# Another fixed order for the 524 interleaved steps of the hybrid mixer

## What is computed

```python
def hybrid_mixer(h, ...):
    proj = h @ w_in
    gq, gk, gv, gate, ga, gb, sq, sk, sv = _split(proj, HYB_SPLITS)
    qkv = causal_short_conv(concat(gq, gk, gv), conv_w)      # 4 heads of 128
    o_a = gated_delta_rule(l2_norm(q), l2_norm(k), v, g, beta)
    o_a = rms_norm(o_a, gdn_norm) * silu(gate)
    o_b = stick_breaking_attention(rms_norm(sq), rms_norm(sk), sv)   # 8 heads of 64
    return concat(o_a, o_b) @ w_out
```

## Time and profile before

| | us |
|---|---|
| runs of the kernel: lowest, median, highest (3 runs) | 2892.62, 2895.24, 2897.87 |
| profiled execution, its span (first to last instruction) | 2890.9 |
| of it the mixer on PE, from its first slab to the output projection | 41.4 to 445.0 |
| the four mixer parts used below | 40 to 155, 155 to 265, 265 to 360, 360 to 445 |

### The profile page before, as it was taken

How to read it: one execution, slowest core, us unless ns; L and a number is a source line. 1 busy time by engine, 2 the same in 40 slices (tenths; PEclk the granted TensorE clock), 3 DMA queues, 4 the chain that set the end, 5 groups by cost and what they waited for, 6 DMA issues and landing times.

```text
span 2890.9 us, 31908 instructions
## 1 busy us (share of the span) xinstructions
PE 2779.2 (96%) x13258; PEld 2203.1 (76%) x13258; DVE 1412.4 (49%) x2062; ACT 961.1 (33%) x1264; POOL 547.4 (19%) x422
## 2 busy tenths in 40 slices
PE   7998989999999999999999999899999998999998
PEld 4776657888887787788888876688888875788886
DVE  6645546666545333373222455555345465454453
ACT  3435444322233322243222333433223344322222
POOL 2563301100112201221001200022012100121121
PEclk9999979999999999999999999899999999999999
DMA  6322103446322222223632322122322321222321
GB/s 242 124 92 93 50 8 146 175 174 226 142 99 99 91 79 86 77 88 102 173 116 70 121 93 71 38 106 84 108 102 71 120 62 62 73 98 79 108 84 69
DMA packets 51089, 296.28 MB, mean 102 GB/s; under 512 B 6618, under 2 KB 6746, under 8 KB 25089
## 3 DMA queue, kind: packets, MB, share of 16 engines
q1 hardware_dynamic: 44912, 276.58, 27.1%
q0 software_dynamic: 4736, 15.34, 2.0%
q10 hardware_dynamic: 1296, 2.32, 0.2%
HBM read 283.46 MB, written 8.65 MB: 101 GB/s over the span
## 4 chain that ended last, share of the span: by engine, by line
PE 88%; DVE 5%; ACT 4%; issue 1%; POOL 1%; DMA 0%; SPq 0%; DVEq 0%
PE ps L218 87%; DVE wlo L211 1%; PE ps L1327 1%; ACT whi L200 1%; DMA F<-in_ada 0%; ACT F L1344 0%; DVE F L418 0%; DVE hl L422 0%; DVE ada L466 0%; DVE F L2270 0%; ACT L253 0%; ACT E L2843 0%; DVE F L833 0%; ACT E L2841 0%; ACT hh L436 0%
## 5 line engine op out<-in xcount | busy, mean ns | idle before, releaser
L218 PE MATMUL ps<-hh,whi 128*128 128x512 f32 x2088 | 829.1, 397 | 12.6 <-ACT F L2821 5.8
L218 PE MATMUL ps<-hl,whi 128*128 128x512 f32 x2088 | 814.9, 390 | 0.0
L218 PE MATMUL ps<-hh,wlo 128*128 128x512 f32 x2088 | 813.9, 390 | 0.0
L211 DVE TENSOR_TENSOR wlo<-raw,whi 128x2048 fp32r<-128x2048 f32 (+2 forms) x235 | 496.2, 2111 | 503.5 <-ACT whi L200 501.3
L218 PE MATMUL ps<-R,whi 128*128 128x512 f32 x2080 | 651.3, 392 | 8.0 <-DVE wlo L211 3.1
L200 ACT ACTIVATE whi<-raw 128x2048 fp32r<-128x2048 f32 (+2 forms) x235 | 409.7, 1744 | 746.8 <-PE ps L218 746.7
L218 PEld LDWEIGHTS ps<-hh,whi 128*128 128x128 f32 x2088 | 392.8, 188 | 103.6 <-issue 12.2
L218 PEld LDWEIGHTS ps<-R,whi 128*128 128x128 f32 x2080 | 391.1, 188 | 95.7 <-issue 6.9
L218 PEld LDWEIGHTS ps<-hl,whi 128*128 128x128 f32 x2088 | 392.6, 188 | 83.4
L218 PEld LDWEIGHTS ps<-hh,wlo 128*128 128x128 f32 x2088 | 393.1, 188 | 82.1 <-issue 3.3
L218 PE MATMUL ps<-R,wlo 128*128 128x512 f32 x1040 | 405.2, 390 | 0.0
(11 more groups left out here) (341 smaller groups left out, 2434.7 us busy)
## 6 DMA issues: line engine op xcount, KB each, us to landing
F<-in_ada SPq DMA_DIRECT2D x32, 1024.0 KB, 4.8
raw<-in_fs0in SPq DMA_DIRECT2D x22, 1024.0 KB, 5.5
raw<-in_fs1in SPq DMA_DIRECT2D x22, 1024.0 KB, 4.8
raw<-in_fc0in SPq DMA_DIRECT2D x22, 1024.0 KB, 4.8
raw<-in_fc1in SPq DMA_DIRECT2D x22, 1024.0 KB, 4.8
Rf<-in_ada0h SPq DMA_DIRECT2D x24, 512.0 KB, 3.5
raw<-in_fs0out SPq DMA_DIRECT2D x16, 704.0 KB, 4.3
raw<-in_fs1out SPq DMA_DIRECT2D x16, 704.0 KB, 4.3
```

Of the source, the lines that this page charges most:

```text
L211: e.tensor_tensor(m.wlo[n % 2][:, 0:size], m.raw[m.slot[n]][:, 0:size], m.whi[n % 2][:, 0:size].bitcast(F32), SUB).then_inc(*s.up("wlo", n))
L218: return e.matmul(out, l, r, start=start, stop=stop, skip_group_check=True)
```

## The change

The greedy schedule is gone. The order is now a table of 524 letters with repeat counts, read from a string. Only the order of steps between chains differs; each chain's own steps, their instructions and buffers are the same, and so is the order of the slabs. The checks of dependencies remain as assertions, and bank 6's users are recorded from the new order.

```diff
-FIRST_CHOICE = ("gates", "heads", "delta0", "delta1", "ada", "stick")
-BEGIN = {"gates": 1.0, "ada": 13.0, "heads": 1.0, "delta1": 20.0, "delta0": 0.0, "stick": 1.0}
+CHAINS = {"d": "delta0", "e": "delta1", "s": "stick", "h": "heads", "a": "ada", "g": "gates"}
+
+ORDER = """
+d9 a g2 a g d4 g d2 g d2 g d2 a d e5 d g e d e g d a e g2 e d s d a s3 d3 e2 a e3 a d2 e3 d e a d s e2 s2 a s e d a s d
...
+e h d e2 h3 d e4 h d e3 d h d e h2 d e h3 e2 h3
+"""
...
-    while any(at[i] < len(chains[i]) for i in chains):
...
-        i = min(start, key=start.get)
-        work, mark, beside, _, done = chains[i][at[i]]
+    at, order, slabs, before, held, last, done = dict.fromkeys(chains, 0), [], [], {}, False, None, set()
+    for i in (CHAINS[word[0]] for word in ORDER.split() for _ in range(int(word[1:] or 1))):
+        _, mark, _, needs, finished = chains[i][at[i]]
+        assert all(n in done for n in needs), (i, at[i])
```

More of the change, by code:

```diff
@@ L2107, in ada_steps @@
         yield step("pe:0.5 dve:0.2", ("six", "mod", "h", j + ADA_BATCH - 1), done="modulation" if j + ADA_BATCH == 40 else None)
-FIRST_CHOICE = ("gates", "heads", "delta0", "delta1", "ada", "stick")
-BEGIN = {"gates": 1.0, "ada": 13.0, "heads": 1.0, "delta1": 20.0, "delta0": 0.0, "stick": 1.0}
+CHAINS = {"d": "delta0", "e": "delta1", "s": "stick", "h": "heads", "a": "ada", "g": "gates"}
+ORDER = """
+d9 a g2 a g d4 g d2 g d2 g d2 a d e5 d g e d e g d a e g2 e d s d a s3 d3 e2 a e3 a d2 e3 d e a d s e2 s2 a s e d a s d
+s e a s d2 e s e2 s2 e2 d e d s2 e s d a s e s e d s e d a d3 e d e d s2 d e a d2 e d2 e d e2 d s d h d e3 d3 h s e h d
+h s2 d a d e h e d e h d2 h d2 s d2 e h e s d e d e2 d s a2 e h2 e h e s d e d e d e h d2 h d2 e h d s2 e a d s d e d h2
+d2 s d a e s e d h e h d e2 d e2 d e h e2 d2 s h e2 d2 e s2 h d a e2 a e d h2 e d2 h e2 d a e h e h e3 h e h e d2 h d a
+h d h e d h2 e2 d2 s h s d2 h2 s3 h d h d s d s d h d s a2 d s3 h e s h2 d e h e s e h a d s d e2 s e h d3 e d e a h e
+d2 h d s d2 h d h e d h d h e d3 h s d s2 h a h e d a h d e h s e a h d e h d e d e2 h d h d e h d e s h d s e2 h s h s
+e s h e d2 h e h2 e s h e2 s e d h s e d e s2 e2 h2 e3 h d e2 h e3 d e h e d e d2 e3 h d e h e h e2 h2 e2 h e2 d e d2 h
+e h d e2 h3 d e4 h d e3 d h d e h2 d e h3 e2 h3
+"""
 def hybrid_order():
@@ L2119, in hybrid_order @@
               "stick": list(stick_steps()), "ada": list(ada_steps()), "gates": list(gate_steps())}
-    at, ready, free = {i: 0 for i in chains}, dict(BEGIN), {"pe": 0.0, "act": 0.0, "dve": 0.0, "pool": 0.0, "dma": 0.0}
-    order, slabs, before, held, last, when = [], [], {}, False, None, {}
-    while any(at[i] < len(chains[i]) for i in chains):
[L2123 to L2128, removed]
-        i = min(start, key=start.get)
-        work, mark, beside, _, done = chains[i][at[i]]
+    at, order, slabs, before, held, last, done = dict.fromkeys(chains, 0), [], [], {}, False, None, set()
+    for i in (CHAINS[word[0]] for word in ORDER.split() for _ in range(int(word[1:] or 1))):
+        _, mark, _, needs, finished = chains[i][at[i]]
+        assert all(n in done for n in needs), (i, at[i])
         if mark and mark[0] == "slab":
+            assert not held, (i, at[i])
             slabs.append(mark[1:])
@@ L2138, in hybrid_order @@
             held = False
[L2139 to L2147, removed]
+        if finished:
+            done.add(finished)
         at[i] += 1
         order.append(i)
+    assert all(at[i] == len(chains[i]) for i in chains)
     return order, slabs, before
```

## The result

The changed kernel takes 2862.95 us (median of 4 runs, 2860.01 to 2866.52) against 2896.55 of the kernel before in the same series (4 runs). The ratio is 0.9891, 95% interval 0.9872 to 0.9909. The predicted time was 2879.5 and its range went down to 2865: the kernel is faster, and the gain is twice the one that was forecast. A later series gave 2862.85 (4 runs) and 0.9894 (0.9878 to 0.9910). In the five series of the experiments 108 runs of the kernel before have a median of 2893.8, so the gain is 31 us. The profiled execution after took 2866.52 us, the highest of its four runs, with a span of 2864.7; the one before took 2892.62, the lowest of its four, with 2890.9. So 1.7 us lie around a span and not 4.3, and the two profiles differ by 26 us only.

The account below looks back on a forecast made before the run. PE, busy 96% of the span, bounds the kernel, so only its waits and half clock in the mixer could be saved. Terms summed to -15.7 us: span 2875.2, plus 4.3 gives 2879.5 us; 80% range 2865 to 2893.

Parts of the forecast that it names:

- the rivals: Full clock in the last part (2871.6 or 2867.6, chance 0.15); waits only change places (2893, 0.13); POOL's slab pairs slower (2911.5, 0.12).
- the last part at the full clock: Mixer's last part: all 11.9 us of half clock return, 2871.6, or 2867.6 with the remaining idle time; chance 0.15.
- The estimate by weight loads: Mixer's last part: by weight-load busy time, 59% against 78% behind it, it could shrink to 64 us, 21 us gained; not adopted.
- -4.3 for the second query-key slab: Its four copies move ahead of a stick head's three ACT passes; PE's 5.33 us wait falls to some 1 us.
- +1.4 for the passages of heads 0 to 2: Passages between PE steps with no other PE work rise from 5 to 8, about 0.48 us of wait each.
- +2 for POOL: Two adaLN slabs between two masks instead of one may delay POOL's masks for PE; +2 us, between 0 and 10.
- -6.9 for the stick heads: Last three stick heads: more PE work between scores and cumulative sum, saving 1.5, 2.4 and 3.0 us.
- -1.9 for passages of head 3: From head 3's first inverse level on, passages without other PE work fall from 11 to 7, about 0.48 us each.
- -4 of clock: Mixer's last part: a third of the 11.9 us that 34 us at half clock cost comes back.
- The third stretch: Third stick head: PE work between scores and sum grows from 5.2 to 6.9 us against a 2.86 us wait; -2.0 us.
- the first: First value slab: its 2.68 us wait for a copy behind ACT's l2 norm of head 0 shrinks; -2.0 us.
- The other new waits, +2: Allowance for waits the old order did not have, as nearly every step moves; +2 us, between 0 and 6.

Follow-up runs that it names:

- the fillers: Unread 128x128 matmuls added late in the mixer: 83 or 36 in the old order, 2895.83 or 2892.11 us; 19 in the new order, 2866.26 us.
- the stretches: Old order with only steps 0-86, 86-271, 271-365 or 365-524 in new relative order: 0.9992, 0.9973, 1.0038 (0.9991 with adaLN slabs put back), 0.9965.
- the run alone: Old order with only its last 159 steps (365 to 524) in the new relative order: 2887.36 us, 0.9965 to the kernel before.
- the run inside the new order: Changed kernel with its last 159 steps in the old relative order, adaLN slabs kept as in the new: 2878.35 us, 0.9944 to the kernel before.
- t1: Old order; in its last 159 steps only delta0 and delta1 take the new order relative to each other: 2899.13 us, 1.0020.
- t2: Old order; in its last 159 steps stick heads, last slab and adaLN steps take new places beside delta1, delta0 and delta1 stay old: 2898.29 us, 1.0021.
- the first searched order: Third order of the same 524 steps, found by exchanging steps and following all engines' waits with trace durations: 2856.30 us, 0.9877 to the kernel before.

## Why the prediction was wrong

**Side and place: right.** Faster was the likeliest outcome, and all but 3 us of the profiled difference lie inside the mixer, which now ends at 421.6, not 429. None of the rivals came about. The nearest in time, the last part at the full clock (2867.6), is half true: its time at the lower clock fell from 34 to 6 us, but 9.0 us idle remain, and the fillers found no gain in that clock. The estimate by weight loads (64 us for the last part) did not come about either: they are busy 35.81 of 61.5 us, 58% against 59% before. What it rests on stands in the Trainium skill's Perfetto Trace Analysis under Identifying the Most-Contended Engine, not under Engine Utilization.

**The step that failed is the middle of the sum**, -4.3 for the second query-key slab with +1.4 for the passages of heads 0 to 2 and +2 for POOL: -0.9 together. The runs gave -7.8 (alone) and -13.0 (in the new order), the ledger -7.4 and -13.8. A second assumption failed with it, that places add up: alone, the stretches give 22.8 of the 31 us.
- The copies were mis-sized. I took the waiting time less 1 us and nothing for what follows a wait. By itself the step is worth 7.8 us (0.9973), 3.5 more than predicted, of which 1.1 is half clock by the estimate above. It was the one large wait in 110 us, and I had put the clock's return in the last part alone.
- The +2 for POOL's pairs was not there as a wait for POOL: the list of PE's waits, which goes down to 0.4 us, has no adaLN slab and no mask. The mechanism exists where two slabs stand directly ahead of their sum (15.27 and 11.03 us). And POOL's slabs reach PE by another way, through DVE (last section).
- The +1.4 was counted by passages with no other PE work. But the lag of the middle fell to 7.3 in one profile and 0.9 in the other, so counting bare passages is no measure of a stretch. The 6.4 us between these two are the clock of the one execution.

**The tail: right as a sum, not shown by parts.** -6.9 for the stick heads, -1.9 for passages of head 3 and -4 of clock gave -12.8, the lag -12.6 and -13.6, the run alone -10.1 and the run inside the new order -14.5. That the sum fits is partly luck. But t1 and t2, priced with the same unit prices at -0.7 and -3.8, came out at +5.8 and +6.1. Each price assumed that everything else arrives as before. For the last head I counted 3.9 us of PE work against a delay of 6.4; its sum now comes 6.8 us after the scores, because some of that work waits on ACT behind the very passes it was to cover.

**The third stretch** (-2.0 predicted, -2.6 run) **and the first** (-2.0, -2.3) are not contradicted, but neither run is clear of no change, and the ledger gives +0.7 for the third and -4.1 or 0.0 for the first. In the first the wait only moved, from 2.68 at the slab to 2.97 at the step ahead of it.

**The other new waits, +2:** they exist (2.84 at delta0's step 122 and 1.73 at its step 103, both for DVE), and the ledger holds them in its net figures.

**The clock, -4.** The half-clock time inside the mixer is 44 us before, and 37 and 24 in the two profiles after, by the 5 us windows. It left the last part (34 to 6 us) and came up in the second and third (7 to 31 us in the first profile). At 0.37 us each the 7 and 20 us less are 3 and 7 us of the 23.4 and 26.7 by which the mixer got shorter, an estimate, and an upper one, since in the old tail the fillers found no gain. Between the medians there is an association: the granted clock averages 0.9868 over the 108 runs before and 0.991 over the 8 after. Among the runs before, 0.001 of mean clock goes with 2.0 us (2899.2 us at 0.984, 2889.8 at 0.989), so 0.0042 goes with about 8 us. It is no price: the old order with 83 fillers has the new order's 0.991 and still takes 2895.83 us. By the rule that I weighed (the Trainium skill, TensorE: Matmul & The Clock Gate, HAM oscillation) denser work keeps the clock up. The trace agrees (0.69 to 1.00 in the window with fillers), but the time doesn't follow when the density is filler.

**The base and the range.** 4.3 us around the span was read off one profile and the median of three runs; it was 1.7, and 2.6 us of the miss in level come from that. The ratio is free of it. The forecast's own range was added up wrongly at its upper end: with its bounds (clock 0, added terms 16) it reaches 2895.5, not 2892. The 80% range began at 2865, and the gain lay below it.

**What stays open:** what decides in one execution whether the clock falls; where the other half of the copies' 7.8 us lies; why the middle is worth 13.0 inside the new order and 7.8 alone; and whether the stick heads or the passages carry the tail's gain, since their halves can't be separated.

## What to carry to other kernels

Don't price a reordering as a sum over single places in the old surroundings: a step is worth what the whole net of queues lets it be worth, and half a good order can be slower than none. Read the one large wait first and move that. When the steps, their waits and their durations can be read from a trace, following all of them for each exchange is worth its while: it found an order 17 us below the new one. Profile the same program twice before a stretch of a few us is explained.

## What the runs showed of the hardware

**DVE passes that read only SBUF wait for POOL.** In the new order the last convolution of head 3 met an adaLN slab. All engines, around the wait of 2.84 us:

```profile
305.17 0.47 DVE L2265 TENSOR_SCALAR F<-raw,cols 128x512 f32<-128x512 f32 x1
...
309.50 0.74 DVE L2268 SCALAR_TENSOR_TENSOR F<-raw,cols,F 128x509 f32<-128x509 f32 x1
...
311.52 2.21 DVE L2265 TENSOR_SCALAR Rf<-Rf,cols 128x512 f32<-128x512 f32 x1 [1.28 <-ACT Rf L2237]
311.55 1.90 POOL L2955 TENSOR_TENSOR Rf<-Rf,csil 128x1024 f32<-128x1024 f32 x1 [6.84 <-DMA Rf<-in_ada0h]
...
313.76 3.63 DVE L2268 SCALAR_TENSOR_TENSOR Rf<-Rf,cols 128x511 f32<-128x511 f32 x3
...
316.80 1.17 POOL L2661 TENSOR_TENSOR F<-F 128x256 f32<-128x256 f32 x1
...
317.31 0.27 DVE L2615 TENSOR_TENSOR F<-F,ps 128x128 f32<-128x128 f32 x1
...
317.73 1.01 PE L218 MATMUL ps<-F 64*64 64x64 f32 x14 [2.84 <-DVE F L2615]
```

A first pass (L2265) takes 0.47 us alone and 2.21 when POOL's 1.90 us product starts beside it; the three that follow take 3.63 us together instead of 0.74 each. The four passes lose 3.15 us so, and PE's wait behind them is 2.84. The subtraction that reads PSUM (L2615) takes 0.27 beside POOL's mask, where its mean over the mixer is 0.28. The wait of 1.51 us has such a pass ahead of it too (L2875, 1.89 us beside POOL's product, 0.68 alone at 237 us), and so has its twin of 1.56 us in the kernel before (L2289, 1.77 and 1.21), where it could have been read before the prediction. The Trainium skill (SBUF — State Buffer, Who interferes with whom) says that the pair of ports which the two share is an exclusive lock, so the later one is blocked for the whole instruction. The trace agrees in that POOL's product takes its usual 1.90 us and DVE's pass ends 0.28 us after it. Which was issued first it doesn't settle: the recorded starts are 0.03 us apart, DVE's ahead. I had not counted this in any term: it is how POOL's slabs did reach PE, through DVE. What it costs in time is not shown; moving the passes away gained nothing (2864.09 us).

**The granted clock varies from run to run of one kernel**, from 0.981 to 0.990 for the kernel before, and with it the time from 2908 to 2886 us. The figure isn't always a measure of speed: one run of the first searched order, the profiled one, shows 0.942 and took 2864.40 us, only 8 more than the median of the other three at 0.992 and 0.993. Behind its mixer, most windows of 5 us show 0.95, and a matmul of 128x512 follows the next every 0.23 us as elsewhere. A profile shows one of these executions, so a difference of under 10 us between two profiles is not yet one between kernels.
